# A two-layer encoder trunk on one core: the second gated half moved ahead of the second queries, the LayerNorm ahead of the second heads' attention

## The chip, the core and the metric

The kernel runs on one core of a Trainium2 chip. The metric is the device time of one execution in microseconds (us). The core's engines run side by side and meet at semaphores: TensorE (PE: matmuls and transposes), VectorE (DVE), ScalarE (ACT), GpSimd (POOL) and SyncE (SP, which here only issues the DMAs). Each engine works its own instruction list strictly in order.

## The reference, cut to what matters

The trunk has two layers on 256 tokens of width 2048, all in float32. The first mixer (the only part that the change touches) is this:

```python
def conv_attention_mixer(h, w_in, w_out, dw_w, dw_b, ln_g, ln_b, qn_g, kn_g, sinks):
    z = h @ w_in
    a, gate, q, k, v = jnp.split(z, [s1, s2, s3, s4], axis=-1)   # widths 1024, 1024, 1024, 128, 128
    u = a * jax.nn.sigmoid(gate)
    u = causal_depthwise_conv(u, dw_w) + dw_b                    # 31 taps, 1024 channels
    u = jax.nn.silu(layer_norm(u, ln_g, ln_b))                   # over the 1024 channels
    q = rms_norm(q.reshape(b, t, N_Q_HEADS, HEAD_DIM), qn_g)     # 16 heads of 64
    k = rms_norm(k.reshape(b, t, N_KV_HEADS, HEAD_DIM), kn_g)    # 2 key heads
    v = v.reshape(b, t, N_KV_HEADS, HEAD_DIM)
    o = banded_sink_attention(q, k, v, sinks)                    # softmax with a sink, band of 128
    return jnp.concatenate([u, o], axis=-1) @ w_out
```

The mixer's result is added to x. A SwiGLU feed-forward part, a short gated convolution mixer and a second SwiGLU part follow; they are the bulk of the time and stay as they are.

## The kernel before, in words

Every weight matrix is streamed from HBM in slots. A slot is 128 partitions x 1024 floats (512 KB): two k-tiles of 512 output columns, or, for the jobs called narrow, four k-tiles of 256 columns. Float32 accuracy comes from splitting each operand into a high and a low part: ACT copies the slot to `w_hi` (a rounded copy, the function `highs`), DVE or POOL computes `w_lo = w_raw - w_hi` (`lows`, `low`), and PE multiplies hi by hi, hi by lo and lo by hi. Wide slots take 12 matmuls of 512 columns, narrow ones 24 of 256. In the mixer the lows of odd slots are POOL's and those of even slots DVE's. There is a ring of four slots (`RING`): ACT writes the high of slot s when PE has used slot s-4.

A job is a run of slots that accumulates into one pair of PSUM banks (one bank for each half of the tokens). There are three pairs; a job starts when the pair's last content has been read. `Plan` numbers the slots, pair uses and transposed groups; the order in which `plan.job` and `plan.group` are called has to be the order of work.

The first mixer before, job by job: `g0`, `a0` (the first 512 gate and value channels, 8 slots each), `kv` (4 narrow slots), `q0` (queries of heads 0 to 7, 8 slots), `q1` (queries of heads 8 to 15, 8 slots), `g1` and `a1` of half 0 and of half 1 (16 narrow slots, the function `late`), 8 jobs `attn_out` of two slots (heads' outputs by w_out: head group 0 or 1, column block 0 to 3, the two groups adding into one pair), and 4 jobs `conv_out` of four slots.

Between slots PE does the small steps of the attention. Attention has four parts hh = 0 to 3: parts 0 and 1 are head group 0 with token halves 0 and 1, parts 2 and 3 head group 1. A part goes `score_products` (PE), `score_rows` (DVE: distance penalty, row maximum), `exps` (ACT), `prob_transposes` (PE), `prob_copies` (ACT), `value_products` (PE), `heads_out` (DVE: division). Queries are normalised by `query_squares` (ACT), `query_sums`, `query_norms` (DVE), turned by `query_transposes` (PE), and copied by `query_copies` (ACT). The heads' outputs are turned (`heads_transposes`) and split into hi and lo.

The causal convolution has 31 taps for each of 8 channel tiles. DVE does 2, 3, 5, 6 and part of 7 (`conv_taps`). For tiles 0, 1, 4 and the rest of 7, ACT makes the product of one tap (`tap_products`) in a ring of `PRODUCTS = 8` places and POOL adds it to `cv` (`add_taps`), 96 adds in all. How many products are due after slot s is `products_by(s)`: two for each slot from `FIRST_TAP` (slot 5 of `kv`, counted on) until the first 62 are out, and two more for each slot from `SECOND_TAPS`, 13 slots after the first slot of `g1`. ACT issues the products of slot s behind the high of slot s; POOL does, behind the low of an odd slot s, the adds of slots s-1 and s.

When every tap is in, `channel_means` (PE), a subtraction (DVE), squares (ACT), `channel_variances` (PE), an inverse root with a correcting step (ACT, DVE), Silu and the hi/lo split follow (the LayerNorm); `conv_out` 0 needs its result. The instruction lists of ACT and DVE are written by hand in slot positions, such as `highs_and_taps(z0 + 7, z0 + 8)`; `z0` is the first slot of `g1` half 0, `ao0` the first of `attn_out`, `co0` (`s0` there) the first of `conv_out`.

```python
            for s in range(1, first_ffn, 2):
                if ON_POOL[s]:
                    low(s)
                add_taps(products_by(s - 2), products_by(s))
```

Of the kernel before, what the change touches and what calls it, by code (L numbers as in the profile page):

```python
# [30 lines left out]
F32 = mybir.dt.float32  # L31
# [5 lines left out]
P = 128  # L37
# [80 lines left out]
def encoder_kernel(nc, x_in, w_in, w_out, sc_in, sc_out, w_gate, w_up, w_down, cols_in, tables_in, out):  # L118
# [75 lines left out]
    plan_queries(0), plan_scores(0), plan_scores(1), plan_probs(0), plan_probs(1)  # L194
    plan_queries(1), plan_scores(2), plan_heads(0)
    plan.group(("u1", 0))
    plan_scores(3), plan_probs(2), plan_probs(3)
    plan.group(("u1", 1))
    plan_heads(1)
# [64 lines left out]
    with ExitStack() as ctx:  # L264
# [29 lines left out]
        with ExitStack() as early:  # L294
            oT_hi = sb("oT_hi", [P, KC, SEQ], F32R, early)
            oT_lo = sb("oT_lo", [P, KC, SEQ], F32R, early)
            cv = sb("cv", [P, KC, SEQ], F32, early)
            products = sb("products", [P, PRODUCTS, SEQ], F32, early)
            q_tok = sb("q_tok", [P, TT, AW], F32, early)
# [4 lines left out]
            dists = sb("dists", [P, P + SEQ], F32, early)  # L304
            uT = sb("uT", [P, KC, PAD + SEQ], F32, early)
# [12 lines left out]
            sb("early_end", [P, 24], F32, early)  # L318
            with ExitStack() as heads:
                scores = [sb("scores0", [P, GQ, P], F32, heads), sb("scores1", [P, GQ, SEQ], F32, heads)]  # L320
                qT = sb("qT", [P, GQ, SEQ], F32, heads)

            with ExitStack() as channels:
                uT_hi = sb("uT_hi", [P, KC, SEQ], F32R, channels)
                uT_lo = sb("uT_lo", [P, KC, SEQ], F32R, channels)
# [20 lines left out]
        ln_sq = q_tok[:, :, :].rearrange("p t (c k) -> p (t c) k", k=SEQ)  # L346
# [133 lines left out]
        def _(sp):  # L480
# [52 lines left out]
            load_job(JOB["q1"][0], w_in, 0, SD, 2 * CC + NB)  # L533
# [3 lines left out]
            for g, nb in OUT_ORDER:  # L537
                load_job(JOB[("attn_out", g, nb)][0], w_out, KC + KC // 2 * g, SH // 2, nb * NB)
            for nb in range(NJ):
                load_job(JOB[("conv_out", nb)][0], w_out, 0, SH, nb * NB)  # L540
# [51 lines left out]
            sp.wait_ge(lo_ready, LOW[("ln", KC // 2 - 1)] + 1)  # L592
            ffn(0)
# [52 lines left out]
        def _(pe):  # L646
# [254 lines left out]
            slots("q1", 0, 5, x_hi, x_lo, last=SD)  # L901
            query_transposes(0)
            slots("q1", 5, 6, x_hi, x_lo, last=SD)
            score_products(0, 0, 2)
            slots("q1", 6, 7, x_hi, x_lo, last=SD)
            score_products(0, 2, 4)
            slots("q1", 7, SD, x_hi, x_lo)
            score_products(1, 0, 2)
# [1386 lines left out]
```

## Time and profile before

| | us |
|---|---|
| median of 3 runs | 2096.84 |
| lowest and highest | 2094.84, 2097.55 |
| the profiled execution's own time | 2092.85 |
| its span, first to last instruction | 2091.0 |
| PE busy in it | 2061.4 (99%) |
| DVE, ACT, POOL busy | 1462.6, 1113.9, 470.7 |

A group row gives: line, engine, operation, output<-inputs, shape, count | busy us, mean ns | idle time just before them and what ended it. A timeline row gives: start, duration, engine, line, operation, names, count, and in brackets the idle time before it with its releaser. Matmuls are pipelined, so PE's rows overlap; its pace is read from start to start. The mixer ends where the feed-forward part's first matmul starts, at 313.05 us of the span.

### The profile page before, as it was taken

What the parts mean: (1) busy time and instruction counts of PE and PEld (TensorE: products, weight loads), DVE (VectorE), ACT (ScalarE), POOL (GpSimd) and SP (SyncE); (2) the same over time, 40 slices, a digit from 0 to 9 for tenths busy, and PEclk for the clock granted to TensorE, in tenths of its full rate; (3) what the DMA queues carried; (4) which work ended last, traced back from release to release, by engine and by line L of the source; (5) the groups of instructions that cost most, each with busy time, mean ns of one, the idle gap of its engine ahead of it and who ended that gap; (6) DMA issues with size and microseconds to landing.
All of it is one profiled execution on the core that took longest, in us unless ns stands there. A gap on an engine that the chain in (4) does not pass through costs nothing.

```text
span 2091.0 us, 24352 instructions
## 1 busy us (share of the span) xinstructions
PE 2061.4 (99%) x9598; PEld 1717.4 (82%) x9598; DVE 1462.6 (70%) x1468; ACT 1113.9 (53%) x1265; POOL 470.7 (23%) x260
## 2 busy tenths in 40 slices
PE   9999899999999999999999999999999999999999
PEld 8888777888888888888888888888888888888887
DVE  5786879955887358873776884578738984389832
ACT  6677566544555445554554554455545554455542
POOL 3776630022000420014211014400140003300033
PEclk9999999999999999999999999999999999999999
DMA  7543455556565565645666555566465555655554
GB/s 250 164 130 110 143 202 171 181 181 212 185 229 170 187 214 194 237 150 175 210 207 199 160 192 189 178 214 234 151 225 197 174 191 191 240 181 181 191 191 162
DMA packets 208450, 394.30 MB, mean 189 GB/s; under 512 B 11344, under 2 KB 21968, under 8 KB 208336
## 3 DMA queue, kind: packets, MB, share of 16 engines
q1 hardware_dynamic: 207760, 392.21, 56.5%
q8 instruction: 76, 1.25, 0.2%
q10 hardware_dynamic: 576, 0.53, 0.1%
q14 instruction: 38, 0.31, 0.0%
HBM read 390.60 MB, written 2.10 MB: 188 GB/s over the span
## 4 chain that ended last, share of the span: by engine, by line
PE 89%; DVE 4%; issue 4%; ACT 2%; POOL 1%; DVEq 0%; ACTq 0%; POOLq 0%
PE pair L664 11%; PE pair L666 11%; PE pair L665 11%; PE pair L747 11%; PE pair L745 11%; PE pair L746 11%; PE pair L730 6%; PE pair L732 6%; PE pair L731 6%; PE tbank L760 2%; DVE w_lo L1597 1%; DVE pair L1752 1%; ACT w_hi L1168 1%; POOL cv L630 1%; DVE s_raw L1994 0%
## 5 line engine op out<-in xcount | busy, mean ns | idle before, releaser
L1168 ACT ACTIVATE w_hi<-w_raw 128x1024 fp32r<-128x1024 f32 x584 | 616.7, 1059 | 612.0 <-PE pair L666 306.6
L1597 DVE TENSOR_TENSOR w_lo<-w_raw,w_hi 128x1024 fp32r<-128x1024 f32 x425 | 539.0, 1270 | 403.1 <-ACT w_hi L1168 402.3
L618 POOL TENSOR_TENSOR w_lo<-w_raw,w_hi 128x1024 fp32r<-128x1024 f32 x159 | 388.1, 2442 | 1605.1 <-ACT w_hi L1168 1605.0
L745 PE MATMUL pair<-w_hi,xT_hi 128*128 128x512 f32 x1040 | 404.7, 389 | 0.4 <-DVE w_lo L1597 0.4
L747 PE MATMUL pair<-w_hi,xT_lo 128*128 128x512 f32 x1040 | 404.7, 389 | 0.0
L746 PE MATMUL pair<-w_lo,xT_hi 128*128 128x512 f32 x1040 | 404.6, 389 | 0.0
L1168 ACT ACTIVATE w_hi<-s_raw 128x1536 fp32r<-128x1536 f32 x182 | 270.9, 1489 | 182.0 <-PE pair L747 125.3
L1597 DVE TENSOR_TENSOR w_lo<-s_raw,w_hi 128x1536 fp32r<-128x1536 f32 x182 | 318.5, 1761 | 62.9 <-ACT w_hi L1168 62.8
L664 PE MATMUL pair<-w_hi,yT_hi 128*128 128x512 f32 x704 | 274.9, 390 | 1.0 <-POOL w_lo L618 1.0
L666 PE MATMUL pair<-w_hi,yT_lo 128*128 128x512 f32 x704 | 274.1, 389 | 0.0
L665 PE MATMUL pair<-w_lo,yT_hi 128*128 128x512 f32 x704 | 273.9, 389 | 0.0
L745 PEld LDWEIGHTS pair<-w_hi,xT_hi 128*128 128x128 f32 x1040 | 195.2, 188 | 41.3 <-DVE w_lo L1597 0.8
L746 PEld LDWEIGHTS pair<-w_lo,xT_hi 128*128 128x128 f32 x1040 | 195.2, 188 | 40.6
L747 PEld LDWEIGHTS pair<-w_hi,xT_lo 128*128 128x128 f32 x1040 | 195.2, 188 | 40.5
L1994 DVE TENSOR_TENSOR s_raw<-s_raw 128x1536 f32<-128x1536 f32 x104 | 182.3, 1752 | 0.0
L664 PEld LDWEIGHTS pair<-w_hi,yT_hi 128*128 128x128 f32 x704 | 132.2, 188 | 28.4 <-issue 1.4
L666 PEld LDWEIGHTS pair<-w_hi,yT_lo 128*128 128x128 f32 x704 | 132.1, 188 | 27.6
L665 PEld LDWEIGHTS pair<-w_lo,yT_hi 128*128 128x128 f32 x704 | 132.2, 188 | 27.2
L1998 DVE TENSOR_TENSOR snap<-pair,snap 128x512 f32<-128x512 f32 x156 | 134.9, 865 | 24.6 <-PE pair L747 24.6
L730 PE MATMUL pair<-w_hi,xT_hi 128*128 128x512 f32 x312 | 123.6, 396 | 0.0
L732 PE MATMUL pair<-w_hi,xT_lo 128*128 128x512 f32 x312 | 121.8, 390 | 0.0
L731 PE MATMUL pair<-w_lo,xT_hi 128*128 128x512 f32 x312 | 121.3, 389 | 0.0
(198 smaller groups left out, 2561.6 us busy)
## 6 DMA issues: line engine op xcount, KB each, us to landing
w_raw<-in_w_down SPq DMA_DIRECT2D x176, 512.0 KB, 4.1
w_raw<-in_w_up SPq DMA_DIRECT2D x110, 512.0 KB, 6.5
w_raw<-in_w_gate SPq DMA_DIRECT2D x110, 512.0 KB, 3.8
w_raw<-in_sc_in SPq DMA_DIRECT2D x72, 512.0 KB, 4.4
s_raw<-in_w_gate SPq DMA_DIRECT2D x44, 768.0 KB, 8.1
s_raw<-in_w_up SPq DMA_DIRECT2D x44, 768.0 KB, 8.4
w_raw<-in_w_in SPq DMA_DIRECT2D x52, 512.0 KB, 4.1
w_raw<-in_w_out SPq DMA_DIRECT2D x32, 512.0 KB, 3.6
```

Of the source, the lines that this page charges most:

```text
L618: nc.gpsimd.tensor_tensor(w_lo[at], raw(o), w_hi[at].bitcast(F32), ALU.subtract).then_inc(w_lo_pool, 1)
L664: nc.tensor.matmul(o, hi(k, t), w_hi[:, r, kk, :], start=first, stop=False)
L665: nc.tensor.matmul(o, hi(k, t), w_lo[:, r, kk, :], start=False, stop=False)
L666: mm = nc.tensor.matmul(o, lo(k, t), w_hi[:, r, kk, :], start=False, stop=end)
L730: nc.tensor.matmul(bank, hi[:, k, :], w_hi[:, r, k, :], start=(start and k == 0), stop=False)
L731: nc.tensor.matmul(bank, hi[:, k, :], w_lo[:, r, k, :], start=False, stop=False)
L732: mm = nc.tensor.matmul(bank, lo[:, k, :], w_hi[:, r, k, :], start=False, stop=(stop and k == SK - 1))
L745: nc.tensor.matmul(b, x_hi(k, t), w_hi[:, r, kk, :], start=(first[t] and kk == 0), stop=False)
L746: nc.tensor.matmul(b, x_hi(k, t), w_lo[:, r, kk, :], start=False, stop=False)
L747: mm = nc.tensor.matmul(b, x_lo(k, t), w_hi[:, r, kk, :], start=False, stop=end)
L1168: nc.scalar.activation(w_hi[:, o % RING, tiles_of(o), :], raw(o), ACT.Copy).then_inc(w_hi_ready, 1)
L1597: nc.vector.tensor_tensor(w_lo[at], raw(o), w_hi[at].bitcast(F32), ALU.subtract).then_inc(w_lo_dve, 1)
```

## The change

The order of jobs in the first mixer becomes: `g0`, `a0`, `kv`, `q0`, then `g1` and `a1` of both halves (pairs 1 and 0 in place of 0 and 1), then `q1`, then `attn_out` of head group 0 alone for its four column blocks, then `conv_out` 0, 1, 3, then `attn_out` (1, 0) and (1, 1), `conv_out` 2, and `attn_out` (1, 2) and (1, 3), which add into the pairs of `conv_out` 2 and 3. The attention parts 0 and 1 now run between the slots of `g1` and `a1`; the means and variances come after six slots of `attn_out`; the transposes of the second queries and the parts 2 and 3 run between the slots of `conv_out` 0, 1 and 3. The number of slots, transposes and matmuls stays; two more results are added into x by DVE (`add_pair`, 9 in the mixer's list in place of 7, and one in the next stage in both). The second queries' root uses the table function that the LayerNorm uses, without a reciprocal. `ln_sq` lies in `products` in place of `q_tok`, SBUF tensors change places, and SP waits for one more semaphore (`o_ready` at 4) before it loads for the feed-forward part. `SECOND_TAPS` is written as before, relative to `g1`, which now starts 8 slots earlier.

```diff
     plan.job("q0", 0, KD)
     plan.group("kT")
+    for h in range(2):
+        plan.job(("g1", h), 1, KD, slot_k=HALF_K)
+        plan.job(("a1", h), 0, KD, slot_k=HALF_K)
     plan.job("q1", 1, KD)
-    for h in range(2):
-        plan.job(("g1", h), 0, KD, slot_k=HALF_K)
-        plan.job(("a1", h), 1, KD, slot_k=HALF_K)
-    OUT_ORDER = ((0, 0), (0, 1), (1, 0), (1, 1), (0, 2), (1, 2), (0, 3), (1, 3))
-    for g, nb in OUT_ORDER:
-        plan.job(("attn_out", g, nb), nb % 2, KC // 2, adds=(g == 1))
+    for nb in range(NJ):
+        plan.job(("attn_out", 0, nb), nb % 2, KC // 2)
+    plan.job(("conv_out", 0), 0, KD // 2, on_vector=True)
+    plan.job(("conv_out", 1), 1, KD // 2)
+    plan.job(("conv_out", 3), 0, KD // 2)
+    plan.job(("attn_out", 1, 0), 2, KC // 2)
+    plan.job(("attn_out", 1, 1), 1, KC // 2)
+    plan.job(("conv_out", 2), 2, KD // 2)
+    plan.job(("attn_out", 1, 2), 2, KC // 2, adds=True)
+    plan.job(("attn_out", 1, 3), 0, KC // 2, adds=True)
...
             sp.wait_ge(lo_ready, LOW[("ln", KC // 2 - 1)] + 1)
+            sp.wait_ge(o_ready, 4)
...
             # PE
+            for nb in range(3):
+                attn_out(0, nb, 0, 2)
             channel_means()
+            attn_out(0, 3, 0, 1)
             channel_variances()
+            attn_out(0, 3, 1, 2)
...
+            first_conv_out(0)
+            query_transposes(1)
+            first_conv_out(1)
+            score_products(2, 0, 2)
+            first_conv_out(2)
+            score_products(2, 2, 4)
+            first_conv_out(3)
+            score_products(3, 0, 2)
+            conv_out(1, 0, 1)
+            score_products(3, 2, 4)
+            conv_out(1, 1, 2)
+            prob_transposes(2, 0, 2)
+            conv_out(1, 2, 3)
+            value_products(2, 0, 2)
+            conv_out(1, 3, 4)
+            prob_transposes(3, 0, 2)
+            conv_out(3, 0, 1)
+            value_products(3, 0, 2)
+            prob_transposes(3, 2, 4)
+            conv_out(3, 1, 2)
+            value_products(3, 2, 4)
+            conv_out(3, 2, 3)
+            heads_transposes(1)
+            conv_out(3, 3, 4)
+            heads_split(1)
...
             # DVE, in the LayerNorm's last part
             for q in range(KC // 2):
+                if q == 0:
+                    add_pair(("attn_out", 0, 2), 2, 2)
                 if q == 1:
-                    lows(ao0 + 18, ao0 + 19)
+                    lows(ao0 + 10, ao0 + 11)
                 if q == 2:
-                    add_pair(("attn_out", 1, 3), 3, 2)
+                    query_norms(1)
```

What stands in POOL's list around the place where the second row of taps begins. Here `cv<-products,cv` is the add of one tap and `w_lo<-w_raw,w_hi` the low of one odd slot. Slots are counted through the whole program, the first of `kv` being 16. Before, from the low of slot 47 on (row 34 is the low of slot 49, where the second row of taps begins):

```order
32 L618 TENSOR_TENSOR w_lo<-w_raw,w_hi 128x1024
33 L630 TENSOR_TENSOR cv<-products,cv 128x256 x4
34 L618 TENSOR_TENSOR w_lo<-w_raw,w_hi 128x1024
35 L630 TENSOR_TENSOR cv<-products,cv 128x256 x6
36 L618 TENSOR_TENSOR w_lo<-w_raw,w_hi 128x1024
37 L630 TENSOR_TENSOR cv<-products,cv 128x256 x7
38 L618 TENSOR_TENSOR w_lo<-w_raw,w_hi 128x1024
39 L630 TENSOR_TENSOR cv<-products,cv 128x256 x4
```

And now, from the low of slot 41 on, where it begins:

```order
26 L635 TENSOR_TENSOR w_lo<-w_raw,w_hi 128x1024
27 L647 TENSOR_TENSOR cv<-products,cv 128x256 x6
28 L635 TENSOR_TENSOR w_lo<-w_raw,w_hi 128x1024
29 L647 TENSOR_TENSOR cv<-products,cv 128x256 x8
30 L635 TENSOR_TENSOR w_lo<-w_raw,w_hi 128x1024
31 L647 TENSOR_TENSOR cv<-products,cv 128x256 x8
32 L635 TENSOR_TENSOR w_lo<-w_raw,w_hi 128x1024
33 L647 TENSOR_TENSOR cv<-products,cv 128x256 x7
34 L635 TENSOR_TENSOR w_lo<-w_raw,w_hi 128x1024
35 L647 TENSOR_TENSOR cv<-products,cv 128x256 x8
36 L635 TENSOR_TENSOR w_lo<-w_raw,w_hi 128x1024
37 L647 TENSOR_TENSOR cv<-products,cv 128x256 x8
```

Two groups (6 and 7) held more than four adds before; now six do (6, 8, 8, 7, 8, 8), because the second row of taps starts while 11 slots of the first are still to come, in place of 3. From the low of slot 41 to the last tap POOL has 60 adds in both lists, with 14 lows before and 10 now.

DVE's list in the LayerNorm's last part, before (`uT_lo<-cv,uT_hi` is the low part that PE's `conv_out` 0 waits for, `xs<-pair` is `add_pair`):

```order
166 L1962 TENSOR_TENSOR cv<-cv,junk 128x512 x4
167 L1972 TENSOR_TENSOR uT_lo<-cv,uT_hi 128x512
168 L1597 TENSOR_TENSOR w_lo<-w_raw,w_hi 128x1024
169 L1972 TENSOR_TENSOR uT_lo<-cv,uT_hi 128x512
170 L1723 TENSOR_TENSOR xs<-pair1,xs 128x512 x2
171 L1972 TENSOR_TENSOR uT_lo<-cv,uT_hi 128x512
```

And now, where `q_tok<-q_tok,qk_r2` is the normalising of the second queries that PE's `query_transposes(1)` waits for:

```order
130 L1977 TENSOR_TENSOR cv<-cv,junk 128x512 x4
131 L1746 TENSOR_TENSOR xs<-pair0,xs 128x512 x2
132 L1989 TENSOR_TENSOR uT_lo<-cv,uT_hi 128x512
133 L1620 TENSOR_TENSOR w_lo<-w_raw,w_hi 128x1024
134 L1989 TENSOR_TENSOR uT_lo<-cv,uT_hi 128x512
135 L1704 TENSOR_TENSOR qk_t2<-qk_r2 128x16
136 L1706 SCALAR_TENSOR_TENSOR qk_t2<-qk_t2,qk_ms2 128x16
137 L1710 SCALAR_TENSOR_TENSOR qk_r2<-qk_t2,qk_r2 128x16
138 L1849 TENSOR_TENSOR q_tok<-q_tok,qk_r2 128x512 x2
139 L1989 TENSOR_TENSOR uT_lo<-cv,uT_hi 128x512
```

An `add_pair` now stands ahead of the first `uT_lo`, and five instructions for the queries ahead of the third.

ACT's list from the second queries' copies on, now (`scores<-scores` are the `exps` of parts 2 and 3, `scaled<-tbank` the `prob_copies`):

```order
158 L1195 ACTIVATE w_hi<-w_raw 128x1024 x3
159 L1339 ACT_TABLE_LOAD
160 L1339 ACTIVATE scores0,den<-scores0,neg_top 128x128 x8
161 L1340 ACTIVATE sink_e<-sink_d 128x8
162 L1195 ACTIVATE w_hi<-w_raw 128x1024 x2
163 L1339 ACTIVATE scores1,den<-scores1,neg_top 128x256 x8
164 L1340 ACTIVATE sink_e<-sink_d 128x8
165 L1247 ACTIVATE scaled<-tbank1 128x512
166 L1247 ACTIVATE scaled<-tbank0 128x512
```

As before, the copies of part 2's probabilities stand behind the exponentials of part 3.

## Rows read from the trace of the kernel before

**Rows 1.** The page: busy time and share of each engine.
```profile
PE 2061.4 (99%) x9598; PEld 1717.4 (82%) x9598; DVE 1462.6 (70%) x1468; ACT 1113.9 (53%) x1265; POOL 470.7 (23%) x260
```
**Rows 2.** Who PE waited for between 86 and 313 us: total us, times, longest.
```profile
PE pair L874 <- ACT scaled L1220: 5.1, 4, 2.5
...
PE tbank L760 <- DVE mixed L1714: 0.3, 1, 0.3
```
**Rows 3.** PE's clock around two stretches: window, PE busy, clock, DMA share, GB/s.
```profile
150.00:152.00 2.00, 2.00 (x12) 0.50 0.81 247
...
196.00:198.00 2.00, 0.00 (x0) 1.00 0.16 61
```
**Rows 4.** POOL's groups between 139 and 251 us.
```profile
L630 POOL TENSOR_TENSOR cv<-products,cv 128x256 f32<-128x256 f32 x60 | 52.0, 886 | 2.9 <-POOL cv L630 0.4
L618 POOL TENSOR_TENSOR w_lo<-w_raw,w_hi 128x1024 fp32r<-128x1024 f32 x14 | 33.5, 2392 | 28.7 <-ACT w_hi L1168 28.6
```
**Rows 5.** POOL's timeline.
```profile
139.13 2.40 POOL L618 TENSOR_TENSOR w_lo<-w_raw,w_hi 128x1024 fp32r<-128x1024 f32 x1 [4.81 <-ACT w_hi L1168]
...
199.68 4.37 POOL L630 TENSOR_TENSOR cv<-products,cv 128x256 f32<-128x256 f32 x4
...
247.83 2.77 POOL L630 TENSOR_TENSOR cv<-products,cv 128x256 f32<-128x256 f32 x4
```
**Rows 6.** PE's timeline, from a run of ten wide slots to the feed-forward part.
```profile
220.49 0.47 PE L664 MATMUL pair<-w_hi,oT_hi 128*128 128x512 f32 x1 [1.47 <-DVE oT_lo L1672]
...
247.81 1.89 PE L986 MATMUL tbank<-cv,ones 128*128 128x256 f32 x8
...
253.18 1.13 PE L986 MATMUL tbank<-cv,ones 128*128 128x256 f32 x4 [2.08 <-DVE cv L1752]
...
266.17 0.50 PE L664 MATMUL pair<-w_hi,uT_hi 128*128 128x512 f32 x1 [2.91 <-DVE uT_lo L1972]
...
313.05 0.39 PE L730 MATMUL pair<-w_hi,xT_hi 128*128 128x512 f32 x1
```
**Rows 7.** PE's small groups over the whole span.
```profile
L874 PE MATMUL pair<-kv_tok,scaled 128*128 128x64 f32 x96 | 12.1, 281 | 5.1 <-ACT scaled L1220 5.1
L844 PE MATMUL tbank<-kT,qT 64*128 64x128 f32 (+1 forms) x64 | 9.0, 349 | 1.1 <-DVE scores L1842 1.1
...
L760 PE MATMUL tbank<-ident,scores 128*128 128x128 f32 x48 | 7.9, 319 | 0.0
...
L760 PE MATMUL tbank<-ident,q_tok 128*128 128x128 f32 x32 | 4.5, 277 | 3.0 <-DVE q_tok L1863 1.5 <-DVE q_tok L1823 0.9 <-DVE scores L1842 0.7
```
**Rows 8.** PE's timeline in part 3 of the attention and the value products of part 2.
```profile
175.62 1.14 PE L844 MATMUL tbank<-kT,qT 64*128 64x256 f32 x8
182.55 1.04 PE L760 MATMUL tbank<-ident,scores 128*128 128x128 f32 x8
187.10 1.97 PE L874 MATMUL pair<-kv_tok,scaled 128*128 128x64 f32 x16 [0.64 <-ACT scaled L1220]
```
**Rows 9.** DVE's timeline: the end of the means, low parts, an add of a pair.
```profile
253.04 0.42 DVE L1739 TENSOR_TENSOR cv<-pair,cv 128x256 f32<-128x256 f32 x1
...
265.43 0.69 DVE L1972 TENSOR_TENSOR uT_lo<-cv,uT_hi 128x512 fp32r<-128x512 f32 x1
266.04 1.22 DVE L1597 TENSOR_TENSOR w_lo<-w_raw,w_hi 128x1024 fp32r<-128x1024 f32 x1
...
267.77 1.28 DVE L1723 TENSOR_TENSOR xs<-pair,xs 128x512 f32<-128x512 f32 x2
```
**Rows 10.** DVE's groups between 86 and 254 us.
```profile
L1752 DVE SCALAR_TENSOR_TENSOR pair<-uT,early_cols,pair 128x256 f32<-128x256 f32 x131 | 55.9, 481 | 1.1
L1597 DVE TENSOR_TENSOR w_lo<-w_raw,w_hi 128x1024 fp32r<-128x1024 f32 x22 | 31.5, 1433 | 19.6 <-ACT w_hi L1168 19.5
...
L1823 DVE TENSOR_TENSOR q_tok<-q_tok,qk_r 128x512 f32<-128x512 f32 x4 | 4.6, 1194 | 0.1
...
L1687 DVE SCALAR_TENSOR_TENSOR qk_r<-qk_t,qk_r 128x16 f32<-128x16 f32 x2 | 3.0, 1485 | 0.1
```

More of the change, by code:

```diff
@@ L203, in encoder_kernel @@
         plan.split(("ln", q))
-    OUT_PAIRS = (0, 1, 2, 0)
-    for nb in range(NJ):
-        plan.job(("conv_out", nb), OUT_PAIRS[nb], KD // 2, on_vector=(nb == 0))
+    plan_queries(1), plan_scores(2), plan_scores(3), plan_probs(2), plan_probs(3)
+    plan_heads(1)
     def plan_sums(norm):
@@ L304, in encoder_kernel @@
             dists = sb("dists", [P, P + SEQ], F32, early)
+            q_tok = sb("q_tok", [P, TT, AW], F32, early)
+            oT_hi = sb("oT_hi", [P, KC, SEQ], F32R, early)
+            oT_lo = sb("oT_lo", [P, KC, SEQ], F32R, early)
+            with ExitStack() as channels:
+                uT_hi = sb("uT_hi", [P, KC, SEQ], F32R, channels)
+                uT_lo = sb("uT_lo", [P, KC, SEQ], F32R, channels)
+            products = sb("products", [P, PRODUCTS, SEQ], F32, early)
             uT = sb("uT", [P, KC, PAD + SEQ], F32, early)
@@ L1928, in _ @@
[L1928 to L1936 removed]
+            taps = conv_taps(U1_TAPS, U1_TAPS + 6)
@@ L1937, in _ @@
+            heads_lows(0)
+            taps = lows_and_taps(z0 + 22, ao0 + 5, taps, 10, ALL_TAPS)
+            add_pair(("attn_out", 0, 0), 0, 2)
+            taps = lows_and_taps(ao0 + 5, ao0 + 7, taps, 10, ALL_TAPS)
+            add_pair(("attn_out", 0, 1), 1, 2)
+            lows(ao0 + 8, ao0 + 9)
             conv_taps(taps, ALL_TAPS)
@@ L1976, in _ @@
             s0 = JOB[("conv_out", 0)][0]
-            at = s0 + 4
-            for nb in range(NJ - 1):
-                done = s0 + SH * (nb + 1)
-                lows(at, done + 3)
-                add_pair(("conv_out", nb), nb, SH)
-                lows(done + 3, done + 5)
-                at = done + 5
-                if nb == 0:
-                    sums_first(1)
-                elif nb == 1:
-                    sums_second(1)
-                else:
-                    x_split(1, nb)
+            add_pair(("attn_out", 0, 3), 3, 2)
+            lows(s0 + 4, s0 + 6)
+            score_rows(2)
+            lows(s0 + 6, s0 + 7)
+            add_pair(("conv_out", 0), 0, SH)
+            lows(s0 + 7, s0 + 8)
+            score_rows(3)
+            lows(s0 + 8, s0 + 11)
+            heads_out(2)
+            add_pair(("conv_out", 1), 1, SH)
+            lows(s0 + 11, s0 + 13)
+            heads_out(3)
+            lows(s0 + 13, s0 + 15)
+            heads_lows(1)
+            lows(s0 + 15, s0 + 17)
+            add_pair(("attn_out", 1, 0), 0, 2)
+            lows(s0 + 17, s0 + 19)
+            add_pair(("attn_out", 1, 1), 1, 2)
+            sums_first(1)
+            lows(s0 + 19, s0 + 21)
+            sums_second(1)
+            lows(s0 + 21, s0 + 25)
+            add_pair(("attn_out", 1, 2), 2, 2)
+            lows(s0 + 25, s0 + 26)
+            x_split(1, 2)
+            at = s0 + 26
             def remake(n, step, dest, a, b):
```

305 lines of the change are left out of this document (135 added, 170 removed).

## The prediction

> **What bounds the kernel now.** I read the page first: PE is busy 2061.4 of 2091.0 us [rows 1], so TensorE is the bound and at most 29.6 us, 1.4%, is idle. Then PE's waits in the mixer. Between 86 and 313 us there are 13 entries, from 5.1 us (four waits of the value products for ACT's copies of the probabilities) down to 0.3 us, 20.0 us in all [rows 2], the first and the last of 13 stand there. The LayerNorm's 2.91 [rows 6] is not touched, nor is the one for the keys; at most 17 us are what the change can get at. Third, the granted clock: twice in this stretch it stands at 0.50, the 1.2 GHz level, for some us, the second time behind a window of 2 us in which PE did nothing [rows 3]; each costs 1 us or more. So about 19 us, 0.9%, is the most that better cover of the attention could bring. Last I looked at who could take PE's place, and read the timelines of POOL and DVE up to the means. POOL has idle time of 28.7 us in front of its lows there [rows 4], which the page's 23% for POOL doesn't tell as a local matter: between 139 and 251 us it is busy 85.5 of 112.
>
> **What the change moves.** No matmul is added or taken. Everything ahead of the means loses eight wide slots (`attn_out` of group 1) and the attention of the second head group; both come back behind the means. A wide slot is 2.73 us: ten of them from 220.49 to 247.81 [rows 6], so eight are 21.9 us. PE's small groups of both head groups add up to 12.1 + 9.0 + 7.9 + 4.5 = 33.5 us [rows 7], 16.8 for one; a piece is about 0.2 us shorter from start to start than its row, and there are 13 pieces: 14 us. So 35.9 us of PE's content pass from ahead of the means to behind them, and the change of the total is: (end of the means now) - (end before) + 35.9 + (waits behind the means now) - (those before). The end before is 253.18 + 1.13 = 254.3 [rows 6]. The feed-forward part begins at 313.05 with no wait between but the 2.91 us for `uT_lo` [rows 6].
>
> **Step 1, the end of the means: POOL.** The convolution must be complete for them. From the low of slot 41 on POOL has 60 adds in both lists (the order shows them: groups of 6, 8, 8, 7, 8, 8 now, mostly 4 before), because the second row of taps starts eight slots earlier while the first row ends where it did. An 8-add group with its low costs 8 x 0.867 + 2.39 = 9.3 us (52.0 over 60, and the mean of a low) [rows 4], and PE asks for an odd slot every two slots, 5.5 us. So POOL can't keep up: it runs without a gap, ACT's products stay at most 8 ahead of it, and PE waits for `w_lo` of odd slots in `q1` and at the means. The end follows from POOL alone: start of the low of slot 41, plus 60 adds at 0.867 (52.0), plus 10 lows at 2.39 (23.9). The start was 139.13 [rows 5]; it hangs on ACT, which first does the exponentials of part 1, and those on DVE's `score_rows(1)`, ahead of which now stand three more taps (3 x 0.43) [rows 10] and a gate multiply of two instructions of a tap's size (0.9): 141.3. Then 141.3 + 52.0 + 23.9 = 217.2. Behind it DVE's last add into `cv` (0.4) [rows 9] and the last matmuls (1): 218.6. Before, POOL ended at 247.83 + 2.77 = 250.6 [rows 5], a little ahead of DVE, after 28.7 us of waiting for ACT. The result of step 1: 218.6 - 254.3 + 35.9 = +0.2 us. The waits of the attention are gone from ahead of the means, and POOL's queue has taken their place: PE's own content would bring it to the means at 247.8 - 35.9 = 211.9 with all old waits, and up to 17 us earlier without.
>
> The unknown of this step is the add. The fastest group of four took 2.77 (0.69 each, 41.5 for 60: 10.5 us earlier), the slowest 4.37 (1.09 each, 65.6: 13.6 us later) [rows 5]. I take the mean of the 60, since DVE beside it does the same taps and lows as before.
>
> On POOL and DVE together: an instruction of 16 elements on DVE took 1.49 us in the mean of two, one of 1024 elements 1.43 [rows 10]; the small one can't be work. The Trainium skill (SBUF - State Buffer, SBUF: two separate sides) says that a GpSimd instruction and a VectorE instruction with two SBUF inputs exclude each other for their whole length. The trace agrees in this row. By that rule a POOL without gaps would also hold up DVE's lows, and the other way round, so that the adds would come nearer to 1.09 than to 0.69; this speaks against the change. By another page (GPSIMD Engine Reference, Elementwise - side-by-side cycle accounting) an add of 2048 elements takes 4.5 us, hence, as an estimate, 0.56 for 256; with it POOL would be done some 18 us earlier and the first rival below would hold. The trace has the add, so it is used.
>
> **Step 2, the first `conv_out` slot.** An `add_pair` of 1.28 us [rows 9] now stands ahead of the first `uT_lo`. `query_sums(1)` ahead of the variances lies in the time in which DVE waits for PE anyway. PE's wait of 2.91 grows by 1.3 us. Nothing covers it: PE has only two slots of `attn_out` here, as before.
>
> **Step 3, the second queries.** PE does one slot (2.73) and then wants the queries. DVE after the first `uT_lo`: a low 1.2, `uT_lo` 0.7 [rows 9], three 16-element instructions and two of 512 elements. The latter took 1.19 each, the small ones up to 1.49 [rows 10] with POOL in the way: 1.9 + 2.4 + 4.5 = 8.8, a wait of 6.1. POOL has little to do here, and a 512-element `uT_lo` takes 0.69: then 1.9 + 1.4 + 0.6 = 3.9, a wait of 1.2. It is near the lower end; I take 1.5.
>
> **Step 4, the value products of part 2.** ACT copies part 2's probabilities only behind the exponentials of part 3. From PE's last scores of part 3 to the value products of part 2 it took 187.10 - 175.62 = 11.5 us, and PE still waited 0.64 at the end [rows 8], so 11.5 is the length of the chain. PE's cover was three narrow slots and two small groups; now it is two wide ones: 1.1 + 2.73 + 0.8 + 2.73 = 7.4. A wait of 4.1, or about 3 where DVE's row maximum isn't held up: 3.3. For the later parts I find cover of a slot or more each; 0.4 in all for the bank of the scores and the split of the heads.
>
> **Costed at nothing:** two more `add_pair` (2.6 us on DVE, which after the means has idle time in front of its lows; without that cover PE would wait as much); SP's wait for `o_ready` 4 (SP reaches it only when slot 80's low is done, long after `heads_out(3)`; were it later, the first loads of the feed-forward part would be late by as much); one slot in place of two between the last transposes and the feed-forward part (up to 1 us). The narrow loads come earlier, with the same bytes.
>
> **Sum.** +0.2 + 1.3 + 1.5 + 3.3 + 0.4 = +6.7 us. The profiled execution took 2092.85 (span 2091.0 and 1.85 around it); it would become 2099.5. The median of the runs is 2096.84, 4.0 above it, and with the same addition 2103.5.
>
> **Rivals.**
> - **POOL is quicker, and the change pays.** If the adds take 0.69 us (the tap of tile 0 and 1 alternate in the dense groups, and DVE does only one low for eight adds), POOL ends 10.5 us earlier. DVE must then be ready too: before, its last tap ended with the add into `cv` at 253.0 [rows 9], 2.4 us behind POOL, with 19.6 us of idle time in front of its lows [rows 10], so it has room for that. With the waits of steps 2 to 4 at half (3.3) it gives 0.2 - 10.5 + 3.3 = -7.0 us: 2089.8. Against it: only groups of four with little beside them ran so fast [rows 5], and the 60 took 52.0. It decides from an add of less than 0.74 us on. It ends on the other side.
> - **The two cancel.** Adds at 0.78, half way to the fastest, and the rest as forecast: 5.2 us less, +1.5: 2098.
> - **It is worse.** Adds at 1.0 (+8), and PE's idle 5 to 10 us at the means and in the LayerNorm bring the clock to 1.2 GHz once or twice behind the means, where nothing hides it (up to 1.7 us each, as the two of before) [rows 3]: about +17: 2114.
> - **The change does nothing** (the order stays bound by PE's content and the waits only move) would be 2097; it falls with the second.
>
> **How the numbers follow.** Forecast 0.50 (own range 2099.5 to 2109), quicker POOL 0.15, cancelling 0.22, worse 0.13. About 0.2%, 4.2 us, is what a measurement tells from no change: faster is below 2092.6, slower above 2101.0. Slower 0.50 + 0.13, same 0.22, faster 0.15. The range goes from 2092 (the first rival's time lies below it) to 2113.
>
> **What would show it.** Right: PE rows of wide slots behind `POOL w_lo` with 3 to 4 us each in `q1`, three or four of them, and 5 us or more at the means for `cv` of POOL; POOL without gaps for 76 us, with mean adds of 0.87; `uT_lo` waited for 4.2; the transposes of `q_tok` waited for 1 to 2 and one wait of 3 to 4 of the value products for ACT. Wrong: POOL with gaps in front of its lows in `q1`; then the forecast falls to the first rival. Wrong too, and slower: a wait of PE for weights from DMA, or at the start of the feed-forward part.

## The result: 10 us slower, 0.5%

The changed kernel takes 2107.22 us in the median (2102.79 to 2107.52), the one before, on the same chip and in turns with it, 2097.2. The ratio is 1.005, 95% interval 1.0037 to 1.0063. The forecast was +6.7, inside a range of 2092 to 2113.

The profiled execution of the changed kernel took 2107.28 (span 2105.5), that of before 2092.85: 14.4 us between the profiles, 10 between the medians. Before's execution lay 4.4 below its own median; the changed kernel's did not. The mean granted clock of each execution goes with that: of the 82 executions of the kernel before that were timed beside the experiments, the 26 at 0.998 took 2092.8 us in the mean, the 15 at 0.996 took 2096.1, and the 24 at 0.994 took 2099.8. The profiled one stood at 0.998; the changed kernel's six stood at 0.991 to 0.993. So every row "of before" comes from an execution in which the clock took little (3.4 us in the mixer, by the rows below), and the differences of profiles below count more of the clock than the medians do.

The page after, answering [rows 1]:

```profile
PE 2071.7 (98%) x9598; PEld 1726.3 (82%) x9598; DVE 1462.7 (69%) x1471; ACT 1113.3 (53%) x1264; POOL 468.5 (22%) x260
```

PE is busy 10 us longer with the same 9598 instructions, and idle 4 us longer. Ten us of extra busy time without an extra instruction point to instructions that ran slower, and the clock's rows below show them. The waits of PE in the mixer, answering [rows 2]:

```profile
PE pair L681 <- POOL w_lo L635: 9.0, 3, 3.6
PE pair L891 <- ACT scaled L1247: 5.1, 2, 2.7
PE pair L681 <- DVE uT_lo L1989: 3.9, 1, 3.9
PE tbank L861 <- DVE scores L1868: 2.3, 2, 1.4
PE tbank L777 <- DVE k_twice L1833: 1.8, 1, 1.8
PE tbank L980 <- POOL cv L647: 1.7, 1, 1.7
```

Where they stand, in PE's timeline, with the means (220.18) and the first matmul of the feed-forward part (330.78), answering [rows 6]:

```profile
153.13 3.34 PE L891 MATMUL pair<-kv_tok,scaled 128*128 128x64 f32 x16 [2.39 <-ACT scaled L1247]
...
190.37 0.50 PE L681 MATMUL pair<-w_hi,xT_hi 128*128 128x512 f32 x1 [2.52 <-POOL w_lo L635]
...
201.30 0.80 PE L681 MATMUL pair<-w_hi,oT_hi 128*128 128x512 f32 x1 [3.59 <-POOL w_lo L635]
...
220.18 2.00 PE L980 MATMUL tbank<-cv,ones 128*128 128x256 f32 x8 [1.69 <-POOL cv L647]
...
235.74 0.80 PE L681 MATMUL pair<-w_hi,uT_hi 128*128 128x512 f32 x1 [3.94 <-DVE uT_lo L1989]
...
265.28 2.90 PE L891 MATMUL pair<-kv_tok,scaled 128*128 128x64 f32 x16 [2.68 <-ACT scaled L1247]
...
319.98 0.50 PE L681 MATMUL pair<-w_hi,oT_hi 128*128 128x512 f32 x1 [2.90 <-POOL w_lo L635]
...
330.78 0.39 PE L747 MATMUL pair<-w_hi,xT_hi 128*128 128x512 f32 x1
```

Two distances serve from here on for every kernel, both read from such rows. **M** is the end of the means, plus 35.9 us where the order is the new one (the content that the prediction found to pass behind them), less before's 254.3: what the stretch ahead of the means costs. **T** is the way from there to the feed-forward part, less before's 58.7 (313.05 - 254.31) and, in the new order, less 35.9: what the stretch behind costs. The changed kernel has M = 222.18 + 35.9 - 254.3 = **+3.8** and T = 108.6 - 58.7 - 35.9 = **+14.0**. Together 17.8; some 3.3 of it are won back later. Of these 2.3 come in the first 25 us of the feed-forward part: 1.1 is a shorter wait for `snap` (1.4 in place of 2.5), 0.6 are two waits for `w_lo` that before has there and the changed kernel hasn't. The last 1.0 gathers evenly over the 1750 us behind (two groups of transposes that stood 42.40 us apart stand 42.38 apart), in code that both kernels share; what makes it isn't known. M and T are each read from one profiled execution, so they hold what the clock took in that one.

POOL ahead of the means, answering [rows 4] and [rows 5]:

```profile
L647 POOL TENSOR_TENSOR cv<-products,cv 128x256 f32<-128x256 f32 x60 | 50.9, 870 | 2.9
L635 POOL TENSOR_TENSOR w_lo<-w_raw,w_hi 128x1024 fp32r<-128x1024 f32 x10 | 23.8, 2384 | 8.5 <-ACT w_hi L1195 8.5
```
```profile
142.53 2.38 POOL L635 TENSOR_TENSOR w_lo<-w_raw,w_hi 128x1024 fp32r<-128x1024 f32 x1 [7.19 <-ACT w_hi L1195]
...
162.25 6.58 POOL L647 TENSOR_TENSOR cv<-products,cv 128x256 f32<-128x256 f32 x8
...
190.28 8.65 POOL L647 TENSOR_TENSOR cv<-products,cv 128x256 f32<-128x256 f32 x8
...
218.04 2.77 POOL L647 TENSOR_TENSOR cv<-products,cv 128x256 f32<-128x256 f32 x4
```

Of the 8.5 us of idle time, 7.19 lie ahead of the first low; POOL then has 1.3 us of waits for ACT in 78 us, against 23.8 in 111 us in the trace of before (its 28.6 less the 4.8 ahead of the first low). The queue forecast is there. DVE at the means and behind them, answering [rows 9]:

```profile
216.90 0.48 DVE L1775 SCALAR_TENSOR_TENSOR cv<-uT,early_cols,pair 128x256 f32<-128x256 f32 x1
220.91 0.42 DVE L1762 TENSOR_TENSOR cv<-pair,cv 128x256 f32<-128x256 f32 x1 [3.53 <-POOL cv L647]
221.25 1.28 DVE L1746 TENSOR_TENSOR xs<-pair,xs 128x512 f32<-128x512 f32 x2
222.45 1.22 DVE L1620 TENSOR_TENSOR w_lo<-w_raw,w_hi 128x1024 fp32r<-128x1024 f32 x1
223.58 2.47 DVE L1960 TENSOR_TENSOR cv<-cv,tbank 128x512 f32<-128x512 f32 x4
...
237.34 0.17 DVE L1704 TENSOR_TENSOR qk_t<-qk_r 128x16 f32<-128x16 f32 x1
...
237.95 1.29 DVE L1849 TENSOR_TENSOR q_tok<-q_tok,qk_r 128x512 f32<-128x512 f32 x2
```

DVE had its own taps done at 217.38 and waited 3.53 for POOL: POOL is last, DVE only 3.5 ahead of it.

The granted clock, answering [rows 3]; columns: window, PE busy, clock, DMA share, GB/s (the busy times of the other engines stand between):

```profile
90.00:94.00 4.00, 4.00 (x11) 3.12 (x10) 4.00 (x9) 0.68 (x2) 4.00 (x3) 0.50 0.81 262
...
154.00:158.00 4.00, 4.00 (x21) 4.00 (x21) 3.41 (x6) 2.67 (x6) 4.00 (x6) 0.50 0.67 184
...
266.00:270.00 4.00, 4.00 (x17) 3.61 (x16) 2.46 (x1) 1.51 (x2) 2.36 (x1) 0.51 0.02 4
270.00:274.00 4.00, 4.00 (x17) 3.23 (x17) 1.77 (x6) 0.23 (x1) 0.00 (x0) 0.63 0.77 248
```

The trace has seven stretches at 1.2 GHz in the mixer, 34.1 us in all, where before's has two of 3.4 us each. Each comes just behind a wait of PE (1.8 to 3.9 us), though not every such wait has one: the 2.91 in [rows 6] has none. Matmuls start half as often there (those of a wide slot every 0.43 us in place of 0.23), so the 13.65 us at 1.2 GHz behind the means (3.4 behind `uT_lo`, 6.8 behind the value products, 3.4 behind slot 21) cost 6.8 us, booked as busy time. The one at 88 us, 6.8 us long, stands in code that both kernels share; it costs 3.4 us. It is absent from before's profiled execution and there (3.4 us long) in that of `e11` below, which has before's order. So it comes and goes with the execution. Most of M = +3.8 is its work: `e12` below, with the same stretch, has M = +4.0, and `e9` and `e13`, which are the same up to slot 41 and haven't the stretch, have +1.0 and +1.2. POOL's low of slot 41 starts at 142.53 in the changed kernel and 3.3 us earlier in `e9`:

```profile
139.24 2.37 POOL L635 TENSOR_TENSOR w_lo<-w_raw,w_hi 128x1024 fp32r<-128x1024 f32 x1 [7.19 <-ACT w_hi L1195]
```

The stretch also counts in the 14.4 between the profiles; how much of it counts in the 10 between the medians isn't known.

### The profile page after: what moved, and what is told of

The parts are those of the page before. It is cut to its first block, busy times and chain, and to the rows that moved or that the text cites. A ratio compares the mean times of both kernels' runs of the same rounds, so it can differ in the third digit from the quotient of the medians.

```text
span 2105.5 us, 24358 instructions
## 1 busy us (share of the span) xinstructions
PE 2071.7 (98%) x9598; PEld 1726.3 (82%) x9598; DVE 1462.7 (69%) x1471; ACT 1113.3 (53%) x1264; POOL 468.5 (22%) x260
## 4 chain that ended last, share of the span: by engine, by line
PE 91%; DVE 4%; issue 2%; ACT 1%; POOL 1%; DVEq 0%; POOLq 0%; ACTq 0%
PE pair L681 12%; PE pair L682 12%; PE pair L683 12%; PE pair L764 11%; PE pair L763 11%; PE pair L762 11%; PE pair L747 6%; PE pair L748 6%; PE pair L749 6%; PE tbank L777 2%; POOL cv L647 1%; DVE w_lo L1620 1%; ACT w_hi L1195 1%; PE pair L891 1%; DVE pair L1775 0%
## 5 line engine op out<-in xcount | busy, mean ns | idle before, releaser
L2024 DVE TENSOR_TENSOR s_raw<-s_raw 128x1536 f32<-128x1536 f32 x104 | 182.0, 1750 | 0.0
```

## The experiments

Each was timed in five rounds against the kernel before, and its ratio is to that. "Taps" means ACT's products with POOL's adds, or DVE's own.

**Is it the convolution?** The first four leave taps out. In `e2` and `e3` tiles 0 and 1 (POOL's) get 16 of 31 taps, in the new order and in before's:

```diff
+        FEW = 16
-        pool_taps = [(c, k) for k in range(TAPS) for c in (0, 1)] + [(4, k) for k in range(SHARE)]
+        pool_taps = [(c, k) for k in range(FEW) for c in (0, 1)] + [(4, k) for k in range(SHARE)]
...
```

> The changed kernel with 30 of the 96 adds left out: channel tiles 0 and 1 get 16 of 31 taps, which leaves part of the convolution uncomputed. POOL has then about 26 us less to do ahead of the means. Theory 1: PE never waits for POOL ahead of the means, and the time falls by 4 to 8 us, to +2 to +6 us; what remains is the part of the loss that lies behind the means. Rival (loss behind the means and in the clock alone): +9 to +10.

> The kernel before with the same 30 adds left out (tiles 0 and 1 get 16 of 31 taps). It tells whether fewer adds pay in any order of work. Theory 1: POOL has 28.7 us of idle time ahead of the means in the order of before, so nothing happens: -2 to 0 us. Rival (fewer adds pay anywhere, since DVE is held up less and ACT has less to do): as much as in the changed order, -4 us or more.

Measured: 2099.0 in the new order, ratio 1.0017 (1.0006 to 1.0027), and 2091.1 in before's, 0.9977 (0.9964 to 0.999). Both gain: by the ratios the new order 7, where its theory had 4 to 8, and the old one 5. That is more than the 0 to 2 of the theory in `e3`; its rival held, fewer taps pay in any order. The two still differ by 8 in place of 10, so POOL alone isn't it. The trace of `e2` says who is next: PE now waits 5.4 us for DVE's `add_pair` ahead of `attn_out` (0,2), which DVE does behind ten taps, without a gap.

```profile
199.57 4.00 DVE L1776 SCALAR_TENSOR_TENSOR pair<-uT,early_cols,pair 128x256 f32<-128x256 f32 x10
203.49 1.27 DVE L1747 TENSOR_TENSOR xs<-pair,xs 128x512 f32<-128x512 f32 x2
```

So `e10` and `e11` do the same for DVE's tiles 2, 3 and 5 as well (45 more taps out), the first in the new order, the second in before's:

```diff
-        dve_taps = [(c, k) for k in range(TAPS) for c in (2, 3)]
+        dve_taps = [(c, k) for k in range(FEW) for c in (2, 3)]
...
-        dve_taps += [(5, k) for k in range(TAPS)]
+        dve_taps += [(5, k) for k in range(FEW)]
```

> The changed kernel with 30 adds of POOL's and 45 taps of DVE's left out: channel tiles 0, 1, 2, 3 and 5 get 16 of 31 taps. Fewer taps of POOL's alone brought +4.0 us, and PE then waited 5.4 us for DVE at attn_out (0,2). Theory (a full DVE stands right behind a full POOL ahead of the means in this order): that wait goes too, the time falls by 3 to 6 us more, to -2 to +1 us against the whole kernel before. Rival (what is left of the loss lies behind the means): +3 to +4 us.

> The kernel before with the same taps left out (tiles 0, 1, 2, 3 and 5 get 16 of 31). The control for the run before it. Theory: in this order DVE's last tap is waited for by 2.1 us at the means, and its lateness in the attention by some more; -8 to -4 us, so the two orders differ by 4 to 6 us when the convolution costs next to nothing, and the rest, 4 to 6 of 10 us, is the convolution's. Rival (DVE hides here): -4 us as with POOL's taps alone, and the orders differ by no more than 2 us.

Measured: 2090.57, ratio 0.9977 (0.9967 to 0.9987), and 2089.74, 0.9969 (0.9958 to 0.9981). The intervals overlap: with a light convolution no difference between the two orders is shown, as the rival in `e11` had it (no more than 2 us). The new order gained more than either guess in `e10`. PE's rows give the split; first the new order, with the end of the means at 202.34 + 3.61 = 205.95, then before's, at 249.74:

```profile
202.34 3.61 PE L981 MATMUL tbank<-cv,ones 128*128 128x256 f32 x16
...
313.75 0.39 PE L748 MATMUL pair<-w_hi,xT_hi 128*128 128x512 f32 x1
```
```profile
248.50 1.24 PE L987 MATMUL tbank<-cv,ones 128*128 128x256 f32 x4 [2.08 <-DVE cv L1753]
...
311.44 0.39 PE L731 MATMUL pair<-w_hi,xT_hi 128*128 128x512 f32 x1
```

| | M | T |
|---|---|---|
| before | 0 | 0 |
| changed | +3.8 | +14.0 |
| `e2`, POOL light, new order | -2.9 | +13.1 |
| `e10`, both light, new order | -12.5 | +13.2 |
| `e11`, both light, before's order | -4.6 | +3.0 |

This is the answer to where the cover of the attention went. Where the convolution doesn't press, the new order reaches the means 7.9 us sooner than the old one, and it pays 10 us behind them. With all the taps it still pays behind the means, and what it should win ahead of them is taken by the convolution on POOL and DVE. ACT's products went with POOL's adds in these runs, so ACT's part of it was not separated.

**Can the taps be spread?** `e1` hands out three taps a slot from the first slot of `g1` on, in place of two and then four:

```diff
-            first = max(0, min(2 * (s - FIRST_TAP + 1), 2 * TAPS))
+            first = max(0, min(2 * (s - FIRST_TAP + 1) + max(0, s - JOB[("g1", 0)][0] + 1), 2 * TAPS))
```

> The changed kernel with one edit: products_by hands out three taps in place of two for each slot of g1 and a1 until the first 62 are out, so POOL and ACT do 11 or 12 of the adds before the low of slot 41, in time in which POOL is idle now, and the groups of 8 adds become groups of 4 to 6. Theory 1 (POOL's queue sets the end of the means): POOL is done some 8 us earlier, PE's waits for w_lo of odd slots in q1 (6.1 us) and for cv (1.7) go; the time comes to +2 to +6 us against the kernel before, where the changed kernel has +10. Rival (the loss sits behind the means, in the attention between the conv_out slots and in stretches at 1.2 GHz): no change, +9 to +10.

Measured: 2112.49, ratio 1.008 (1.0063 to 1.0096), 17 above before and 5 to 6 above the changed kernel. The theory (+2 to +6) and the rival (+9 to +10) both missed. PE's waits for POOL in `q1` are gone, as was expected, and others stand in their place:

```profile
PE pair L891 <- ACT scaled L1247: 9.7, 2, 7.1
PE pair L681 <- DVE xs L1746: 5.4, 1, 5.4
```

ACT does the extra products while PE wants the first half's probabilities (7.1 us), and the means end at 232.15 (M = +13.7, T = +11.9). The adds earlier in the program hit the attention there. In the 12 us ahead of the copies ACT also waits 3.9 us for POOL's adds, in six pieces, since its ring of products is full; which of the two, products or adds, costs more was not separated. POOL is done at 224.31 here and PE waits for nothing at the means: its last wait ahead of them, 5.4, is for DVE, as in `e2`.

**What do the waits behind the means cost?** Three edits of order, one for each:

`e4` (ACT: part 2's copies ahead of part 3's exponentials):

```diff
+            prob_copies(2, 0, 2)
             exps(3)
-            prob_copies(2, 0, 2)
```

`e5` (DVE: an `add_pair` ahead of the last tap and not of the first `uT_lo`):

```diff
-            taps = lows_and_taps(ao0 + 5, ao0 + 7, taps, 10, ALL_TAPS)
+            taps = lows_and_taps(ao0 + 5, ao0 + 7, taps, 9, ALL_TAPS)
             add_pair(("attn_out", 0, 1), 1, 2)
+            add_pair(("attn_out", 0, 2), 2, 2)
...
-                if q == 0:
-                    add_pair(("attn_out", 0, 2), 2, 2)
```

`e6` (ACT: the high part of slot 21 of the stage ahead of the second sums of x):

```diff
-            highs(s0 + 19, s0 + 21)
+            highs(s0 + 19, s0 + 22)
```

`e9` has all three, `e7` all three and the taps of `e1`. `e9` ran before the single ones.

> The changed kernel with the three edits behind the means alone, taps as they are: part 2's probabilities copied ahead of part 3's exponentials (PE's wait of 2.7 us), the pairs of attn_out (0,1) and (0,2) added ahead of the last tap (2.5 us of the LayerNorm's chain), the high of slot 21 of the conv_out stage ahead of the second sums (2.9 us). Theory (the waits behind the means are a sum of their own, beside POOL's queue): all three are paid back, 8 us: +1 to +4 us against the kernel before, where the changed kernel has +10. Rival (they turn into other waits or the clock takes them): +6 to +10.

> The changed kernel with four edits of order: the evener taps of e1_even_taps; ACT copies part 2's probabilities ahead of part 3's exponentials; DVE adds the pairs of attn_out (0,1) and (0,2) into x ahead of the last tap, in its idle time, in place of ahead of the centring and of the first uT_lo; ACT writes the high of the slot 21 of the conv_out stage ahead of the second sums. Theory 1 with its tail: 6 us from POOL, 2.7 from the copies, 2.5 from the pairs, 2.9 from the high, 14 us in all: -6 to -1 us against the kernel before. Rival (the attention's small matmuls keep the clock low behind the means whatever waits): the four gain half of that, +2 to +5.

> The changed kernel with one edit alone: ACT's copies of part 2's probabilities ahead of part 3's exponentials. In the three edits together (2100.1, 7 us below the changed kernel) the value products' wait of 2.7 behind the means is gone. If each wait behind the means is on the path by itself, this one pays 2.5 to 3: 2104.5. Rival: the clock pays, not the wait (the changed kernel has 6.8 us at 1.2 GHz right there, from 266 us on, and the three edits have none): up to 3.4 more, 2101. If the gain of the three came from one of the others, nothing: 2107.

> The changed kernel with one edit alone: DVE adds the result of attn_out (0,2) into x ahead of its last tap and not ahead of the first low part of the LayerNorm. The prediction's step 2 priced this add at 1.3 us, the profile of the changed kernel shows 3.94 for uT_lo in place of 2.91: a gain of 1.0, 2106. Rival: the add now stands ahead of the last tap, where DVE only just has time before POOL's end; then it moves the means by up to 1.3 and the gain is nothing, 2107.

> The changed kernel with one edit alone: ACT makes the high part of slot 21 of the conv_out stage ahead of the second sums. It takes away PE's wait of 2.9 for the low part of that slot and may take the 3.4 us at 1.2 GHz behind it with it (1.7): a gain of 2.9 to 4.6, 2102.5 to 2104.5. Rival: the transposes of x, now waiting for the sums' results, take over the wait at the start of the feed-forward part: a gain of 1 or less, 2106.

| | us | ratio to before | M | T |
|---|---|---|---|---|
| changed | 2107.22 | 1.005 (1.0037 to 1.0063) | +3.8 | +14.0 |
| `e4` copies | 2100.83 | 1.002 (1.0011 to 1.003) | +3.0 | +8.2 |
| `e5` add_pair | 2107.14 | 1.0049 (1.0036 to 1.0063) | +3.9 | +11.8 |
| `e6` high | 2103.41 | 1.0033 (1.002 to 1.0045) | +2.9 | +10.3 |
| `e9` all three | 2100.14 | 1.0022 (1.0011 to 1.0033) | +1.0 | +6.9 |
| `e7` and even taps | 2104.66 | 1.004 (1.0024 to 1.0055) | +13.3 | +4.8 |

`e4` takes away a wait of 2.7 us and gains 6. The clock is the rest: the two windows that stood at 0.51 and 0.63 read

```profile
266.00:270.00 4.00, 4.00 (x23) 3.40 (x22) 3.86 (x5) 2.07 (x4) 2.27 (x2) 1.00 0.28 87
270.00:274.00 4.00, 4.00 (x32) 3.75 (x31) 2.46 (x5) 2.14 (x3) 1.67 (x1) 1.00 0.77 225
```

The wait of 2.7 and half of the 6.8 us at 1.2 GHz are 6.1; the profiles' T fell by 5.8, the ratio by 0.3%, 6.3 us. The rival of that run, the clock, held: all six profiles with a wait of 2.7 at this place have a stretch behind it, the four without the wait have none (table at the end). In `e6` 2.9 for the low part went, 2.1 for the transposes of x came in, and the stretch at 1.2 GHz behind went too: 0.8 and 1.7 make 2.5, against 3.6 by the ratio. The clock's part of this isn't firm, since `e7`, `e9` and `e13` have the same edit and the stretch stays in them. The 3.7 by which the T of `e6` fell hold 1.7 more that the edit didn't bring: the stretch behind the value products was 3.4 us long in that execution in place of 6.8. In `e5` `uT_lo` is waited for 2.9 again, but the means are waited for 2.7 in place of 1.7: the gain of 1.0 was only handed on, as its rival had it, and nothing is left in the time.

Together the three give 5.9 by the ratio, not the 10 of their sum. Each interval reaches 2 to 3 us to either side, and the runs don't tell why. `e9` ends at +4.6 by the ratio, just above its theory (+1 to +4) and below its rival. Its profile shows what is left: of T = +6.9, 5.1 are the clock (a stretch of 6.8 us from 230 us on and one of 3.4), and 2.1 the wait for the transposes of x. This execution lay 3.6 below its median, that of `e13` 3.4. `e7` was the large miss: -6 to -1 was expected, +2 to +5 by its rival, and it is +8, since the early taps of `e1` cost about as much ahead of the means (M 9.5 above the changed kernel's) as the edits of order bring behind them (T 9.2 below).

**Is it the clock by itself?** `e12` leaves the order alone. It fills two idle places with small matmuls into a bank that nobody reads; `e13` is `e9` with the same fill. The nine matmuls took 2.17 us and the six 1.50, less than the 3.6 and 2.4 that were expected, so of the wait for `uT_lo` 1.93 us stayed idle in `e12`.

```diff
+            def fill(n):
+                for _ in range(n):
+                    nc.tensor.matmul(pairs[2][0][:, 0:P], ones[:, :], ones[:, :], start=True, stop=True)
+            fill(9)
             first_conv_out(0)
...
+            fill(6)
             value_products(2, 0, 2)
```

> The changed kernel with dummy matmuls in two of PE's waits behind the means: 9 of 128x128 (some 3.6 us) ahead of the first conv_out slot, where PE waits 3.9 us for uT_lo, and 6 (2.4 us) ahead of part 2's value products, where it waits 2.7. Nothing of the computation changes. Theory (TensorE's clock goes to 1.2 GHz because PE was idle just before): the half-speed stretches behind these two places, 3.4 and 6.8 us long, go, and the time falls by 3 to 5 us, to +5 to +7. Rival (the small matmuls and single waits have nothing to do with it): no gain, +10 to +11.

> The three edits together with the idle places filled: nine small matmuls into an unused bank in front of the first slot of conv_out and six in front of the value products of part 2. The fill alone paid 3 us (2104.1), the three edits 7 (2100.1). If the fill pays by the clock behind the means, where the three edits still show 6.8 us at 1.2 GHz from 230 us of the span on, both add: 2097, the same as before. Rival: the clock behind the means has its rest from the wait at the means themselves, and the fill only delays PE: 2100 to 2101.

Measured: `e12` 2104.14, ratio 1.0039 (1.0026 to 1.0052); `e13` 2099.64, 1.0015 (1.0005 to 1.0025). The changed kernel's clock was 0.92 and 0.96 in these two windows, `e12`'s is 0.96 and 0.98:

```profile
225.00:270.00 45.00, 41.16 (x218) 33.26 (x217) 33.29 (x64) 30.18 (x68) 7.15 (x3) 0.96 0.33 107
270.00:345.00 75.00, 71.98 (x355) 60.06 (x354) 51.11 (x56) 37.90 (x52) 17.60 (x7) 0.98 0.49 162
```

Its T is +11.5, 2.5 below the changed kernel's, and `e13`'s is +6.2, 0.7 below `e9`'s. By the ratio `e12` is 8 above before, between its theory (+5 to +7) and its rival (+10 to +11); `e13`'s 2099.64 lies at its rival's 2100 to 2101. The intervals of the ratios overlap in both pairs, so the fill's gain in the time itself is likely for `e12` and not shown for `e13`. What the profiles show is the first place: the stretch behind `uT_lo` is there in all six profiles with the unfilled wait of 3.94, and in neither filled one. At the second place `e12` still has 3.4 us at 1.2 GHz, as four of the six unfilled ones do, so nothing is shown for the fill there. In `e13` that place is no longer idle, since the copies come first, and the six matmuls only delay PE by 1.3 us:

```profile
257.57 1.50 PE L1008 MATMUL pair<-ones 128*128 128x128 f32 x12
258.90 1.90 PE L891 MATMUL pair<-kv_tok,scaled 128*128 128x64 f32 x16
```

`e13` is the best of the new order (M = +1.2, T = +6.2), and still slower than before; nothing that computes the whole result beat the kernel before.

## Why the prediction held, step by step

- **The bound.** PE's content and the few waits around it: held. What was not in it is that content can grow without an instruction, by the clock. The 17 us "at most" should have been 15: the 1.8 for the keys was named as untouched but not taken off.
- **Step 1, +0.2; measured +3.8.** The mechanism held: POOL without gaps, last at the means. The add was taken as 0.867 us; its row gives a mean of 0.870, and 50.9 us for all 60. The start, taken as 141.3, was 142.53, and the last add ended at 220.81 and not 217.2. Start, adds and lows as measured give 142.53 + 50.9 + 23.8 = 217.2, the same sum by chance (a later start, shorter adds); the term left out is the pauses in such a chain, 1.3 of waits and 2.9 between adds by the group rows (less some overlap). The late start is the stretch at 1.2 GHz at 88 us: without it the start is 139.24, with 139.13 before, so the 2.2 added for DVE's taps were not seen, and M is about +1 (`e9`, `e13`). The waits on the way were smaller than forecast, 2.5 and 3.6 in place of three or four of 3 to 4, and 1.7 at the means in place of 5 or more: PE arrived later than the prediction let it, held by the value products at 153 and three stretches at 1.2 GHz. As POOL sets the end, that cost nothing more.
- **Step 2, +1.3; measured +1.0** (3.94 against 2.91). Held, but `e5` shows that the us isn't to be had by moving the add.
- **Step 3, +1.5; measured 0.** With POOL idle the three 16-element instructions took 0.17 each and the queries 1.9 in all; PE did not wait. The lower bound was the better guide. The last half us is the clock's doing: PE's slot ahead of them ran at 1.2 GHz, and in `e5`, where it did not, PE waited 0.51 for `q_tok`.
- **Step 4, +3.3; measured 2.7,** and 3.4 more by the clock behind it. `e4` confirms both. For later parts 0.4 was allowed, and PE waited for none of them; the waits for the scores (2.3 in the mixer, 1.1 before) lie ahead of the means, where POOL sets the end.
- **Costed at nothing:** slot 21 of the `conv_out` stage. The prediction asked what covers two more `add_pair` and the shorter way to the feed-forward part, up to 1 us, and did not ask what ACT's second sums put off: the high part started at 316.44 behind them, POOL's low behind that, and PE waited 2.9 and lost 1.7 by the clock. `e6` confirms the cause of the wait.
- **The clock, costed at nothing in the forecast and at 3.4 in the worse rival: 6.8 behind the means.** This is the term that was mis-sized most. [Rows 3] showed that a wait can bring it, and the waits forecast behind the means should have had 1.7 us or more added for most of them. Ahead of the means it has a second part, the stretch at 88 us in M.
- **The sum.** +6.7 against +10 is right in sign and near in size. It is less good than it looks: steps 3 and 4 were too dear by 2.1, step 1, slot 21 and the clock too cheap by 3.6, 2.9 and 6.8, and 3.3 came back behind the mixer; these lead to the profiles' 14.4, which the medians don't reach. That the errors nearly cancel is luck.
- **The rivals.** Quicker POOL fell: the adds took 0.870 and not below 0.74. Even in `e10`, where the means come 12.5 early, T = +13 takes it all back. "Worse" had the right mechanism for the clock with the wrong cause, since the adds did not slow down.

The Trainium skill (SBUF - State Buffer, SBUF: two separate sides) was weighed against the change by the rule that POOL and some DVE instructions exclude each other. With POOL gapless the trace agrees again on DVE's side, as a 16-element instruction ahead of the means took 2321 ns and the same kind 0.17 us at 237 us with POOL idle:

```profile
L1775 DVE SCALAR_TENSOR_TENSOR pair<-uT,early_cols,pair 128x256 f32<-128x256 f32 x131 | 55.8, 480 | 1.1
L1620 DVE TENSOR_TENSOR w_lo<-w_raw,w_hi 128x1024 fp32r<-128x1024 f32 x18 | 28.4, 1578 | 16.6 <-ACT w_hi L1195 16.6
...
L1710 DVE SCALAR_TENSOR_TENSOR qk_r<-qk_t,qk_r 128x16 f32<-128x16 f32 x1 | 2.3, 2321 | 0.0
```

On POOL's side it made no difference to the sum: the adds' mean went from 886 to 870 ns [rows 4], while DVE's lows went from 1433 to 1578 [rows 10].

## What to carry to other kernels

When work is moved so that a result is due earlier, add up what the side engines must finish by then, each alone and without gaps; the time the bound engine saves ahead of that point is theirs first. A wait on TensorE of some us is to be priced with what the clock may take behind it, here 1.7 to 3.4 us where it took anything, which made a copy ahead of the next part's exponentials worth 6 us where the wait was 2.7. Compare profiles only after seeing how each stands to its own median, and what clock each was granted.

## What the runs showed of the hardware

- What a stretch at 1.2 GHz costs appears as PE being busy. Of the changed kernel's T of 14.0 us, the rows of waits show 7.0 (1.0 more for `uT_lo`, 2.7, 2.9, and 0.4 for `xs`), the clock 6.8.
- Such a stretch doesn't come in each execution. The one at 88 us, in code that no kernel here changes, lasted 6.8 us in the changed kernel, `e2`, `e7` and `e12`, 3.4 in `e1`, `e4`, `e5`, `e6`, `e10` and `e11`, and was absent from before, `e3`, `e9` and `e13`.
- How often one stood behind the same wait, over the 14 profiles:

| PE's wait behind the means | profiles with it | with a stretch behind |
|---|---|---|
| `uT_lo`, 3.9 us, not filled | 6 | 6 (3.4 us each) |
| `uT_lo`, 2.9 | 6 | 3 (`e3`, `e9` 6.8, `e11` 3.4) |
| `uT_lo`, filled down to 1.9 and 0.9 | 2 | 0 |
| value products of part 2, 2.7 | 6 | 6 (3.4 or 6.8) |
| the same place without a wait | 4 | 0 |
| low part of slot 21, 2.9 | 7 | 7 (3.4 or 6.8) |
| transposes of x in its place, 2.1 | 4 | 3 (3.4 each) |

- A group of eight adds on POOL took between 6.52 and 8.65 us from its start to its end in the changed kernel: 6.52 and 6.58 with 9 and 10 instructions of DVE beside it, 7.74 and 8.65 with 17 and 16. The runs don't show more of the cause.
